# Two more places for gathered rows in the second context step, and two pauses in the tile computed ahead of the last latent step

## What is computed

```python
def peer_ffn(h, lp):          # 8 heads, 128 keys per half, 16 picks per head
    q = (xt @ lp["peer_wq"]).reshape(n_tok, PEER_HEADS, 2, PEER_HALF)
    s = jnp.einsum("thmd,mhnd->thmn", q, lp["peer_keys"])
    v1, i1 = lax.top_k(s[:, :, 0], PEER_TOPK)
    v2, i2 = lax.top_k(s[:, :, 1], PEER_TOPK)
    ...
    g = jax.nn.softmax(top_s, axis=-1)
    act = jnp.einsum("td,thkd->thk", xb, u_tab[ib])
    out = jnp.einsum("thk,thkd->td", jax.nn.gelu(act) * gb, v_tab[ib])
```

## Time and profile before

| | |
|---|---|
| median of three runs | 2466.62 us (2462.47 to 2470.57) |
| the profiled execution | 2465.23 us, its span 2463.4 us |
| busy: PE, DVE, POOL, ACT | 1674.9, 1570.1, 977.2, 344.0 us |
| moved by DMA | 969.40 MB, mean 394 GB/s |
| gathers (queue q0) | 805.37 MB |
| the chain that ended last | DMA 41%, DVE 25%, PE 24%, issue 5% |

### The profile page before, as it was taken

One profiled execution on the slowest core, in us unless ns is written; L12 is line 12 of the kernel. 1 busy time (PEld: TensorE's weight loads), 2 busy tenths in 40 slices (PEclk: granted clock), 3 DMA queues, 4 the chain that ended last, 5 costly groups with the idle time before them and its releaser, 6 DMA issues.

```text
span 2463.4 us, 20933 instructions
## 1 busy us (share of the span) xinstructions
PE 1674.9 (68%) x6740; PEld 667.5 (27%) x6740; DVE 1570.1 (64%) x4471; ACT 344.0 (14%) x973; POOL 977.2 (40%) x1028
## 2 busy tenths in 40 slices
PE   5899758895566566576755697789556556555564
PEld 2455533470123121122321164347011001110110
DVE  0239985879744556654477588687985555655555
ACT  1321143110000121110001114311000000000000
POOL 0004537547432233332323463764753333333330
PEclk8889888997688777788877898999667777787877
DMA  8989999999999899899997999999999999999996
GB/s 358 400 341 352 410 418 409 413 411 386 414 416 423 324 409 413 361 421 391 404 366 270 392 413 389 391 412 362 384 419 422 422 421 421 422 421 422 422 421 273
DMA packets 164319, 969.40 MB, mean 394 GB/s; under 512 B 18122, under 2 KB 20554, under 8 KB 88690
## 3 DMA queue, kind: packets, MB, share of 16 engines
q0 software_dynamic: 147456, 805.37, 80.5%
q1 hardware_dynamic: 16754, 162.70, 16.0%
HBM read 964.85 MB, written 3.15 MB: 393 GB/s over the span
## 4 chain that ended last, share of the span: by engine, by line
DMA 41%; DVE 25%; PE 24%; issue 5%; ACT 3%; POOL 1%; SPq 0%; DVEq 0%; POOLq 0%; ACTq 0%
DMA ring<-peer_uv_in,vidx 18%; DMA work<-peer_uv_in,vidx 12%; PE acc L1122 6%; DMA wring<-peer_uv_in,vidx 6%; PE psum L825 5%; DVE ring L1981 4%; PE psum L835 2%; DVE work L1534 2%; PE psum L1070 2%; DVE work L1531 2%; DMA ring<-peer_uv_in,idx 2%; PE psum L1046 1%; DVE work L1539 1%; PE acc L1144 1%; PE acc L751 1%
## 5 line engine op out<-in xcount | busy, mean ns | idle before, releaser
L734 POOL DMA_INDIRECT ring<-peer_uv_in,vidx x401 | 382.7, 954 | 605.7 <-PE acc L1122 469.4
L1122 PE MATMUL acc<-ring,vw 128*32 128x512 f32 x924 | 309.4, 803 | 278.5 <-DVE vw L1948 278.5
L1968 DVE CUSTOM_DVE_ANT_0 ring<-ring,h_kept 128x1024 f32<-128x1024 f32 x231 | 280.0, 1219 | 233.0 <-DMA ring<-peer_uv_in,vidx 202.9
L1122 PE MATMUL acc<-work,vw 128*32 128x512 f32 x876 | 295.4, 797 | 190.5 <-DVE vw L1948 190.5
L1968 DVE CUSTOM_DVE_ANT_0 work<-work,h_kept 128x1024 f32<-128x1024 f32 x219 | 265.8, 1219 | 186.9 <-DMA work<-peer_uv_in,vidx 180.9
L734 POOL DMA_INDIRECT work<-peer_uv_in,vidx x256 | 245.5, 959 | 311.6 <-PE acc L1122 257.6
L734 POOL DMA_INDIRECT ring<-peer_uv_in,idx x193 | 183.3, 950 | 341.1 <-DVE idx L1644 208.3
L1981 DVE CUSTOM_DVE_ANT_0 ring<-ring,h_kept 128x1024 f32<-128x1024 f32 x193 | 225.2, 1216 | 15.7 <-DMA ring<-peer_uv_in,idx 14.5
L1433 ACT ACTIVATE dots<-dots 128x2 f32<-128x2 f32 x256 | 52.0, 203 | 1120.3 <-DVE dots L1968 1120.2
L1122 PEld LDWEIGHTS acc<-ring,vw 128*32 128x32 f32 x924 | 52.7, 130 | 511.3 <-DVE vw L1948 374.7
L825 PE MATMUL psum<-wring,work 128*128 128x512 f32 (+1 forms) x432 | 170.9, 552 | 11.7 <-ACT work L1217 8.3
(11 more groups left out here) (251 smaller groups left out, 2015.1 us busy)
## 6 DMA issues: line engine op xcount, KB each, us to landing
wring<-w_in_in SPq DMA_DIRECT2D x17, 2048.0 KB, 10.8
wring<-peer_wq_in SPq DMA_DIRECT2D x14, 2048.0 KB, 10.4
wring<-mod_w_in SPq DMA_DIRECT2D x10, 2048.0 KB, 13.3
ring<-mod_w_in SPq DMA_DIRECT2D x9, 2048.0 KB, 10.2
wring<-w_out_in SPq DMA_DIRECT2D x8, 2048.0 KB, 11.6
work<-mod_w_in SPq DMA_DIRECT2D x5, 2048.0 KB, 14.4
ring<-peer_uv_in,vidx POOLq DMA_INDIRECT x401, 11.6
ring<-w_in_in SPq DMA_DIRECT2D x3, 2048.0 KB, 23.8
```

The lines of the kernel that those rows point to most:

```text
L734: nc.gpsimd.indirect_dma_start(row(kind, k, t, r)[0], None, io["peer_both" if kind == "f" else "peer_one"], bass.IndirectOffsetOnAxis(ap=a ...
L1122: ins = mm(acc[half][lane:lane + QUAD, :], vw_duo(i)[:, j * QUAD:(j + 1) * QUAD], held[:, D + half * CHUNK:D + (half + 1) * CHUNK], start= ...
L1968: V.tensor_tensor_reduce(held[:, 0:D], held[:, 0:D], h_kept[:, :], 1.0, 0.0, ALU.mult, ALU.add, dots[:, at:at + 1]).then_inc(u_used, 1)
```

## The change

The second context step gets two more double places. `region(10288, ...)` is cut into two lines of four instead of three and four, for which `work` grows by 280 columns; that gives one. The other is `lent_line`, a new buffer of two lines that takes in what `vw` and `mod_norms` were. It may hold rows from row (1, 8) of tile 0 on, so POOL waits there for the last sums of the context step, and for the modulation. It serves again in the last stretch, where `work` gives one more as well: 19 instead of 17.

For this the weight blocks of the latent steps move into `cond`, whose content is used up by then, and there are three of them instead of eight. The gates of the latent steps move there too.

The five duos at the head of the last ten move into `tile_ahead`: two behind the product `q`, three behind `k`, and on ACT behind their carries. `region(2 * D, 8 * D)` opens eight rows later, with row (1, 117), and POOL's wait for "picked" moves there with it. The first line of four closes one row earlier, with row (1, 108). From (1, 108) to (1, 116) there are then eight double places, from (1, 117) twelve.

The diff also has code for products and pauses cut into halves. `self.halved` is false everywhere, and with it every such branch gives the sequence of before, names and weights too. It is left out below.

```diff
-VW_DUOS = SHARE // DUO
+VW_DUOS = 3
+LENT_ROW, LEFT_ROWS = 8, 8
+BESIDE_AHEAD = 2, 3
...
-        vw = [sb(f"vw{n}", SHARE * QUAD) for n in range(2)]
-        work = sb("work", 18200)
+        lent_line = sb("lent_line", 2 * D)
+        vw = [lent_line[:, n * SHARE * QUAD:(n + 1) * SHARE * QUAD] for n in range(2)]
+        work = sb("work", 18480)
...
-        mod_norms = sb("mod_norms", 2 * CHUNK)
+        mod_norms = lent_line[:, D:2 * D]
...
-        def vw_duo(i):
-            at = i % VW_DUOS * DUO * QUAD
-            return vw[0][:, at:at + DUO * QUAD]
+        def vw_duo(k, t, i):
+            at = 2 * PICKS + (t * DUOS + i) % VW_DUOS * DUO * QUAD
+            return cond[:, at:at + DUO * QUAD]
...
-        spare_line(region(10288, 3 * D), 3, after_step[STEPS - 3], after_step[STEPS - 2])
-        spare_line(region(10288 + 3 * D, 4 * D), 4, after_step[STEPS - 3], row_no["u", STEPS - 2, 0, 0])
-        spare_line(region(2 * D, 8 * D), 8, after_step[STEPS - 2], row_no["u", STEPS - 2, 0, 0])
+        left_from = ahead_from + LEFT_ROWS
+        spare_line(region(10288, 4 * D), 4, after_step[STEPS - 3], ahead_from - 1)
+        spare_line(region(10288 + 4 * D, 4 * D), 4, after_step[STEPS - 3], row_no["u", STEPS - 2, 0, 0])
+        spare_line(region(2 * D, 8 * D), 8, left_from, row_no["u", STEPS - 2, 0, 0])
...
-        spare_line(region(0, 16 * D), 16, after_step[STEPS - 1], len(stream))
+        spare_line(region(0, 18 * D), 18, after_step[STEPS - 1], len(stream))
...
-        spare([mod_norms[:, :]], lent_from[3], len(stream))
+        line_from = {k: row_no["f", k, 0, LENT_ROW] for k in (1, 3)}
+        spare_line(lent_line, 2, line_from[1], row_no["u", 2, 0, 0])
+        line = range(len(slots) - 2, len(slots))
+        extra.append((line[1:], lent_from[3], row_no["f", 3, 0, 0]))
+        extra.append((line, line_from[3], len(stream)))
...
         left_by = {after_step[STEPS - 3]: ("picked", STEPS - 3, 1),
-                   after_step[STEPS - 2]: ("picked", STEPS - 2, 0),
+                   left_from: ("picked", STEPS - 2, 0),
...
+                for k_line in (1, 3):
+                    if n == line_from[k_line]:
+                        pool.wait_ge(v_used, sums_of(k_line - 1, 0))
+                        pool.wait_ge(*after("mod_whole", "next"))
...
                 project(st, "q", CHUNK, only=0)
+                yield ("ahead", 0)
                 project(st, "k", CHUNK, only=0)
+                yield ("ahead", 1)
...
                     carry(st.L.qk[0][:, where_to:where_to + 512], bank(name, st.k, 0)[:, :], name, st.k, 0)
+                    yield ("ahead", where_to // 512)
...
-                if i >= VW_DUOS:
-                    dve.wait_ge(v_used, used_after["f", k, t, (i - VW_DUOS + 1) * DUO - 1])
+                if t * DUOS + i >= VW_DUOS:
+                    t_before, i_before = divmod(t * DUOS + i - VW_DUOS, DUOS)
+                    dve.wait_ge(v_used, used_after["f", k, t_before, (i_before + 1) * DUO - 1])
...
+            for i, duos in enumerate(BESIDE_AHEAD):
+                upto = ends[-1 - BEHIND_CONTEXT + sum(BESIDE_AHEAD[:i + 1])]
+                plan["ahead", i] = left[most:upto]
+                most = upto
             plan[None] = left[most:]
```

More of the change, by code:

```diff
@@ L827, in project, with project_halves @@
                     ins.then_inc(*made(*jk))
+            def project_halves(st, name, n, point):
+                if not st.halved:
+                    project(st, name, n)
+                    return
+                k = st.k
+                pe.wait_ge(*chunk_landed(name, k))
+                w = chunk(name, k)
+                p = job(pe, name, k, 0)
+                for b in range(DB):
+                    if b == DB // 2:
+                        yield ("half", point)
+                    ins = mm(p[:, 0:n], st.L.hT[0][:, b, 0:P], w[:, b, 0:n], start=(b == 0), stop=(b == DB - 1))
+                ins.then_inc(*made(name, k, 0))
             def conv_project(st, blocks, key):
@@ L832, in conv_project @@
                 for i, bb in enumerate(blocks):
+                    if st.halved and i == 2:
+                        yield ("half", 4)
                     p = job(pe, "xb", st.k, bb)
@@ L856, in opening @@
                 pe.wait_ge(*taken("hT1", k, T - 1, 1))
-                project(st, "q", CHUNK, only=behind)
+                if st.halved:
+                    yield from project_halves(st, "q", CHUNK, 0)
+                else:
+                    project(st, "q", CHUNK, only=behind)
                 yield ("in", 0)
-                project(st, "k", CHUNK, only=behind)
+                if st.halved:
+                    yield from project_halves(st, "k", CHUNK, 1)
+                else:
+                    project(st, "k", CHUNK, only=behind)
                 yield ("in", 1)
@@ L1078, in dense @@
                         key_scores(0, i)
+                    if st.halved and b in WQ_HALVES:
+                        yield ("wq half", WQ_HALVES.index(b))
                     if b in WQ_POINTS:
@@ L1266, in dense @@
                 for b in range(4):
+                    if st.halved and b == 2:
+                        yield ("half", 4)
                     middle_tap(st, b)
@@ L1280, in dense @@
                 yield "dt"
+                if st.halved:
+                    yield ("half", 5)
                 for t in range(T):
@@ L1680, in opening @@
                 yield "h"
-                yield ("in", 0)
-                yield ("in", 1)
+                for i in range(2):
+                    if st.halved:
+                        yield ("half", i)
+                    yield ("in", i)
             def dense(st):
                 k, T, N = st.k, st.T, st.N
+                if st.halved:
+                    yield ("half", 2)
                 yield ("in", 2)
@@ L1906, in dense @@
                 for i in range(4):
+                    if st.halved and i < len(WQ_HALVES):
+                        yield ("wq half", i)
                     yield ("wq", i)
@@ L2046, in pauses_of, with by_half, in_half @@
     names = []
+    def by_half(half, whole, weight):
+        return [(half, weight / 2), (whole, weight / 2)] if st.halved else [(whole, weight)]
+    def in_half(i, weight):
+        return by_half(("half", i), ("in", i), weight * T)
     if not st.early:
-        names += [("start", 0), ("h", 5 * T)]
-        names += [(("in", i), w * T) for i, w in enumerate((10, 7))]
-    names += [(("in", 2), 7 * T), ("rope", 0)]
-    names += [(("in", i), w * T) for i, w in ((3, 4.5), (4, 7))]
-    names += [("dt", 4), (("in", 5), 7 * T), ("conv", 7), ("xw", 9)]
+        names += [("start", 0), ("h", 5 * T)] + in_half(0, 10) + in_half(1, 7)
+    names += in_half(2, 7) + [("rope", 0), (("in", 3), 4.5 * T)] + in_half(4, 7)
+    names += [("dt", 4)] + in_half(5, 7) + [("conv", 7), ("xw", 9)]
     for t in range(T):
@@ L2059, in pauses_of @@
         names += [(("part", t), 7 if t == 0 else 5), (("mid", t), 7 if t == 0 else 5)]
-    names += [(("wq", i), (10 if i == 0 else 7) * T) for i in range(4)]
+    for i in range(3):
+        names += by_half(("wq half", i), ("wq", i), (10 if i == 0 else 7) * T)
+    names += [(("wq", 3), 7 * T)]
     for t in range(T):
```

51 lines of the change are left out of this document (32 added, 19 removed).

## The result

| | before | after |
|---|---|---|
| median of six runs each | 2463.62 us (2457.89 to 2470.57) | 2442.47 us (2438.29 to 2450.46) |
| the profiled execution, its span | 2465.23, 2463.4 us | 2443.51, 2441.7 us |
| start of the context step to its end (below) | 768.7 us | 751.8 us |
| its last gates to its end | 60.0 us | 60.0 us |

The ratio of after to before is 0.9913 [0.9894, 0.9933]: 21 us faster, against 2448 us forecast.

A forecast was written before the change was run, and what follows sets the result against it. The prediction took gather transfers, full rate 422 GB/s, to bound the kernel, with idle time where places ran out in the second context step. 2465.2 - 19.4 + 0.8 = 2446.6 us, as a median 2448; range 2435 to 2459.

The forecast's parts named there:

- The forecast case: Whole kernel: places beside the second context step pay, the end of the choice doesn't; 2441 to 2453 us, chance 0.58.
- Part 1, the five places: Idle stretches near 820, 890, 1010, 1120 and 1210 us, second context step: two more places win 19.4 us.
- a microsecond of idle transfer that is avoided is a microsecond of the step: Second context step: between pauses engines catch up and transfers set the pace, so the 19.4 us avoided count in full.
- Part 2, the end of the choice: End of expert choice and tile ahead: early rows' gain is lost behind row 116; 0.8 us later, bounds +6 and -5.
- The rival that this end pays: End of the choice: up to 15.2 us of POOL's wait come on top, 2433 to 2441 us; chance 0.12.
- The 3.4 us at risk: Product `k` behind a gap and narrow products: a lower clock could stretch it from 6.8 to 10.2 us; counted nothing.
- Part 3, the blocks: Latent steps' weight blocks, three instead of eight: cost nothing, since PE waits for DVE; bounds 0 and 39 us.
- The rival's 39 us: Context step's 15 long pauses: short ring holds DVE, 2.6 us each, 39 us lost, 2486 us; chance 0.07.
- Not the bound: Context step: avoided idle transfer time returns as longer DMA waits, dense work sets the end; 2463 to 2470 us, chance 0.08.
- Half of it: Context step: only two or three of five places count in full; 8 to 14 us, 2453 to 2459, chance 0.15.

The follow-up runs named there:

- e6: The changed kernel run once more, nothing edited: 2446.85 us, ratio to before 0.9943.
- the second pair: Second profiled executions of the kernel before and the changed kernel, neither edited: 766.5 and 752.2 us between the marks of the context step.
- e10: Changed kernel with the ten places but without the pauses, duos back behind the opening: 2443.35 us, ratio to before 0.9922.
- e9: Changed kernel with the lent context buffers open one row earlier, from row (1, 116): 2436.48 us, ratio to before 0.9891.
- e12: Changed kernel with nine double places instead of ten beside the context step: 2451.3 us, ratio to before 0.9956.
- e11: Changed kernel with eight double places again, pauses and three weight blocks kept: 2466.59 us, ratio to before 1.0009.
- e1: Changed kernel with the ten places but without the pauses, on the slower chip: 2594.1 us, ratio to before there 0.9927.
- e4: Changed kernel with the lent context buffers open from row (1, 116), on the slower chip: ratio to before there 0.9869.
- e2: Changed kernel with eight double places again, pauses kept, on the slower chip: 2598.0 us, ratio to before there 0.994.
- e3: Changed kernel with nine double places instead of ten, on the slower chip: ratio to before there 0.9914.

## Why the prediction was right

The forecast was 2448 us, measured was 2442.47, and 2446.85 in e6. The forecast case is the one that came: the places pay, the end of the choice doesn't. The closeness of the number is in part luck: 18.6 us were forecast for the step, which won 16.9 and 14.4. That the first total is below the forecast nevertheless is scatter: before's median fell from 2466.62 to 2463.62 us with three more runs, and the profiled execution of after opened the step 4.5 us early.

**Part 1, the five places.** 19.4 us of idle time forecast, 19.5 and 18.3 measured up to the choice. By places it agrees less well: at 820 to 850 us the rates above leave 2.9 + 4.0 + 3.5 = 10.4 us idle. Before had 5.4 in the first and, from these rows of before,

```profile
830.00:840.00 10.00, 8.35 (x15) 2.21 (x14) 3.81 (x8) 0.00 (x0) 2.53 (x3) 0.50 0.69 224
840.00:850.00 10.00, 8.77 (x24) 3.33 (x22) 1.92 (x5) 0.89 (x3) 0.42 (x2) 0.93 0.70 248
...
1030.00:1040.00 10.00, 5.09 (x23) 1.27 (x19) 5.88 (x17) 1.36 (x6) 5.68 (x7) 0.97 0.96 375
```

4.7 + 4.1, so 3.8 us were won of 5.0. At 1010 it was 3.8 + 0.8 = 4.6 against 3.1 + 4.8 + 1.1 with the third of these rows: 4.3 of 5.0. The places at 890, 1120 and 1210 are gone, 9.4 of 9.4. That makes 17.5; the 2.0 us that it lacks came from small dips that the prediction didn't list, between 630 and 700 us (1.4 us in before, none in after) and elsewhere. In the second pair the five places went from 27.9 to 14.3 us, 13.6 less; 1.4 us are left at 1120. Another 4.3 us came from dips at 690 and 1065. So that the sum came out to 0.1 us in the first pair is luck; that the places shrink by up to a row's transfer for each place is what both pairs show.

**The step that was off** is "a microsecond of idle transfer that is avoided is a microsecond of the step". 19.5 us were avoided and 16.9 won. The transfers up to 94 us ahead of the gates, all and those of the gathers' queue, first in before and then in after, give the difference:

```profile
DMA packets 33009, 244.94 MB, mean 398 GB/s; under 512 B 3639, under 2 KB 4151, under 8 KB 4535
q0 software_dynamic: 30281, 220.49, 87.0%
...
DMA packets 33147, 245.99 MB, mean 411 GB/s; under 512 B 3649, under 2 KB 4161, under 8 KB 4545
q0 software_dynamic: 30419, 221.54, 89.4%
```

The 1.05 MB more are one double row, 2.5 us, that lies ready when the choice begins (1.7 MB and 4 us in the second pair). The choice goes at DVE's pace (one wait for a landing), so a row that is ready early shortens nothing there, and its time comes back as idle time behind (2.9 us more in the two columns). No run isolates this. That is the term to be taken off when the last stretch before a mark is not bound by transfers: what the queue is ahead by at that point.

**Part 2, the end of the choice.** Which row waits and for what was right, and its time to 0.2 us. The end is 60.0 us in both kernels (60.2 and 59.9 in the second pair); 57.6 without the pauses (e10). +0.8 was forecast; these say that the pauses cost nothing to 2.4 us, inside the scatter of the medians. The rival that this end pays needed row 116 to get a place sooner; e9 gives it one and shows the size, 6 us.

**The clock.** The granted clock of the stretch that holds `q` is 0.73, and within the product its rows of weight loads change from one in 0.85 us to one in 0.43 us after 6 us: the lower level first, then the full one. `k` behind a gap of 2.72 us and two duos of narrow products took

```profile
1347.38 7.13 PE L845 MATMUL psum<-wring,work 128*128 128x512 f32 x16
```

7.13 us, the full level throughout, as in one run behind `q` before (16.93 us for both the earlier trace rows). The 3.4 us at risk were not lost in `k`. But the clock did fall, on the narrow products ahead of it:

```profile
1342.00:1345.00 3.00, 2.84 (x8) 0.69 (x10) 2.96 (x8) 0.20 (x1) 0.64 (x1) 0.52 0.00 0
1345.00:1348.00 3.00, 3.00 (x12) 0.72 (x9) 2.00 (x4) 0.00 (x0) 2.18 (x3) 0.91 0.64 161
```

Behind `q`, which ended at the full level, and the gap of 2.72 us, the granted clock is 0.52, the lower level, and the first duo's eight products take from 1342.16 to 1345.73, 3.6 us; those of the second take 1.88 us, and `k` finds the full level. So the low level cost about 1.7 us, on the duo that frees row 108's place, and was over before `k`. In before the first duo behind both products, after a gap of 2.66 us, started at that level too (four products in 1.92 us from 1370.44); in after the one behind `k` runs at the full level (eight in 1.91 us from 1355.75). The price moved with the gap more than it was added. The Trainium skill ("TensorE: Matmul & The Clock Gate", "Why this matters for your kernels") says that gaps between bursts bring the clock down; this trace agrees, only the price fell on other products than the prediction had looked at. `q`, behind a gap of 2.62 us and sparse work, started low in both kernels.

**Part 3, the blocks.** Nothing, as taken: PE's weight load waits for DVE in 237 of 256 duos (236 before) and DVE never for PE. The rival's 39 us were wrong as a price too: even one block costs about 3 at most.

**The rivals.** "Not the bound" falls with the step's 16.9 and 14.4 us. "Half of it" (8 to 14 us, since only two or three places count in full) falls less clearly: all five shrank and three closed in the first pair, but the 14.4 us and 0.9943 of the second lie at its edge. In e12 one place gives about half.

## What to carry over

Count outstanding transfers in units of their own time, and cut the profile where the queue runs dry: one more place is worth at most one row's transfer in each pause that outlasts the store, at most what that pause leaves idle, and probably nothing for the rows that lie ready when an engine-bound stretch begins. Where places are taken in order by an in-order queue, follow the one row that heads the wait: seven rows early gained nothing here, and letting the eighth take another place gained 6 us with an edit of one digit. And when buffers are scarce, ask how many the consumer really leaves standing: three weight blocks served as well as eight (e11 against before), and two as well as three.

## What the hardware showed that I had not expected

The same kernel took 2463.62 us on one chip and 2613.84 us on another, 6% more. The traces of e1 to e4 from the slower one have long waits that no other trace here has, put down to no engine of the core. Two of them, a group of waits of e1 and DVE's last multiplication of the step in e4:

```profile
ACT work L1233 <- remote: 90.8, 10, 17.2
```

```profile
1451.04 1.30 DVE L2076 TENSOR_TENSOR acc<-acc,mod_g 128x512 f32<-128x512 f32 x2 [10.27 <-remote]
```

What they wait for is open. Ratios on that chip were ordered otherwise for e2 and e3 than on the faster ones, by more than their intervals in the case of e2, and what came behind the step varied from 470.5 us (e3) to 493.4 (e1) there. So an edit worth half a per cent should be judged on a chip like the one whose trace was read, and by marks around the stretch that it changes.
